# Output projection by column halves, the first tile's ranks, picks and gather moved up, residual sums opened inside expert 0

## The reference

```
x = x + merged @ w_o                                  # 1024 x 1024
h2 = rmsnorm(x, norm2_g)
logits = h2 @ w_router + b_router                     # 32 experts
top_v, top_i = top_k(logits, 4); gates = softmax(top_v)
for each expert e, for the tokens that chose it:
    gu = h2 @ w_gate_up[e] + b_gate_up[e]             # 1024 x 2048
    act = (clip(gu[1024:], -7, 7) + 1) * g * sigmoid(1.702 * g),  g = min(gu[:1024], 7)
    x += gates * (act @ w_down[e] + b_down[e])        # 1024 x 1024
out = rmsnorm(x, final_g)
```

## Time and profile before

| what | value |
|---|---|
| time, median of 3 runs | 1134.14 us (1133.83 to 1134.21) |
| the profiled execution's own time | 1134.09 us |
| span of its trace | 1132.3 us, mean granted TensorE clock 0.991 |
| PE busy | 1091.9 us, 96% of the span |
| PE weight loads | 482.5 us, 43% |
| DVE, ACT, POOL busy | 223.8, 125.4 and 30.3 us |
| moved by DMA | 434.61 MB, mean 384 GB/s |
| SP's queue | 430.33 MB, 90.1% of what 16 engines can do in the span |
| PE idle for a load of up weights | 20.2 us, 14 times |

### The profile page before, as it was taken

How to read it: one execution, slowest core, us unless ns; L and a number is a source line. 1 busy time by engine, 2 the same in 40 slices (tenths; PEclk the granted TensorE clock), 3 DMA queues, 4 the chain that set the end, 5 groups by cost and what they waited for, 6 DMA issues and landing times.

```text
span 1132.3 us, 12526 instructions
## 1 busy us (share of the span) xinstructions
PE 1091.9 (96%) x5278; PEld 482.5 (43%) x5279; DVE 223.8 (20%) x549; ACT 125.4 (11%) x271; POOL 30.3 (3%) x43
## 2 busy tenths in 40 slices
PE   7999999999999999999999999999999999999996
PEld 5858887443333333333333333333333333333332
DVE  1264213331111111111111121111111111111112
ACT  1053111210000000000000010000000000000001
POOL 1250000000000000000000000000000000000000
PEclk9999999999999999999999999999999999999999
DMA  9934366399999999999999999999999999999995
GB/s 362 411 144 168 130 222 233 144 396 421 432 432 432 429 431 433 431 432 433 432 431 431 435 428 429 439 428 429 438 428 431 435 429 431 434 429 431 417 421 232
DMA packets 31484, 434.61 MB, mean 384 GB/s; under 512 B 6944, under 2 KB 7200, under 8 KB 9440
## 3 DMA queue, kind: packets, MB, share of 16 engines
q1 hardware_dynamic: 26960, 430.33, 90.1%
q10 hardware_dynamic: 4496, 3.87, 1.1%
HBM read 433.14 MB, written 1.05 MB: 383 GB/s over the span
## 4 chain that ended last, share of the span: by engine, by line
PE 65%; DMA 32%; DVE 1%; ACT 1%; issue 0%; POOL 0%; DVEq 0%; SPq 0%; POOLq 0%
DMA ring<-in_up 32%; PE ps L1352 26%; PE ps L1366 11%; PE ps L1172 5%; PE ps L1300 3%; PE ps L1374 3%; PE ps L1186 2%; PE ps L1249 2%; PE ps L1061 2%; PE ps L1361 2%; PE ps L1116 1%; PE ps L1080 1%; PE ps L1051 1%; PE ps L1336 1%; PE ps L1330 1%; PE ps L1089 1%
## 5 line engine op out<-in xcount | busy, mean ns | idle before, releaser
L1352 PE MATMUL ps<-ring,work 128*64 128x512 f32 x2048 | 470.7, 605 | 20.2 <-DMA ring<-in_up 20.2
L1352 PEld LDWEIGHTS ps<-ring,work 128*64 128x64 f32 x2048 | 141.8, 138 | 317.8 <-issue 283.8
L1366 PE MATMUL ps<-ring,work 128*64 128x512 f32 x1024 | 226.8, 595 | 1.6 <-DVE work L977 1.6
L918 DVE TENSOR_SCALAR work<-ps 128x512 f32<-128x512 f32 x32 | 22.1, 691 | 698.1 <-PE ps L1352 698.1
L1366 PEld LDWEIGHTS ps<-ring,work 128*64 128x64 f32 x1024 | 70.6, 137 | 133.7 <-issue 128.0
L1300 PEld LDWEIGHTS ps<-work 128*128 128x128 f32 x512 | 61.8, 191 | 24.0 <-issue 22.7
L1300 PE MATMUL ps<-work 128*128 128x128 f32 x512 | 70.3, 281 | 0.5 <-DVE work L904 0.5
L1374 PE MATMUL ps<-work 64*128 64x512 f32 x264 | 65.6, 615 | 0.7 <-ACT work L658 0.7
L1172 PE MATMUL ps<-work,ring 128*128 128x256 f32 x256 | 56.6, 379 | 0.0
L631 ACT ACTIVATE work<-ps 128x256 f32<-128x256 f32 x33 | 12.7, 383 | 355.5 <-PE ps L1336 355.5
L1172 PEld LDWEIGHTS ps<-work,ring 128*128 128x128 f32 x256 | 48.5, 190 | 6.6
(11 more groups left out here) (157 smaller groups left out, 520.9 us busy)
## 6 DMA issues: line engine op xcount, KB each, us to landing
ring<-in_up SPq DMA_DIRECT2D x52, 4096.0 KB, 45.2
ring<-in_down SPq DMA_DIRECT2D x26, 4096.0 KB, 44.1
ring<-in_up SPq DMA_DIRECT2D x48, 1024.0 KB, 10.8
ring<-in_down SPq DMA_DIRECT2D x24, 1024.0 KB, 10.6
ring<-in_front SPq DMA_DIRECT2D x22, 1024.0 KB, 17.2
ring<-in_front SPq DMA_DIRECT2D x2, 832.0 KB, 7.5
ring<-in_x SPq DMA_DIRECT2D x2, 512.0 KB, 4.2
ring<-in_x ACTq DMA_DIRECT2D x1, 1024.0 KB, 4.8
```

The source lines that it names most:

```text
L918: return dve.tensor_scalar(up_c, ps[:, UP, :], LIMIT, -LIMIT, ALU.min, ALU.max)
L1352: last = pe.matmul(ps[n * CAP:(n + 1) * CAP, bank, :], x, w[bank - GATE][:, n * BANK:(n + 1) * BANK], start=k == 0, stop=k == KT - 1, skip ...
L1366: last = pe.matmul(ps[n * CAP:(n + 1) * CAP, Y, :], lhs(actT, k), w[:, n * BANK:(n + 1) * BANK], start=k == 0, stop=k == KT - 1, skip_grou ...
```

## The change

1. `w_o` is packed by column halves: its first two slots hold half 0, four steps k each, the next two half 1. PE runs half 0 of tile 0, half 0 of tile 1, half 1 of tile 0, half 1 of tile 1. The transposes, the router's products and `add_parts(0)` stand between these passes, at new places, and DVE's and ACT's steps follow the new order: `x2_ready` now counts by half and then by tile. The first two slots of `w_o` are freed in the second pass, the other two in the fourth. The router's partial sums of tile 1 go to bank 0.
2. The counts of tile 0 are made after its own choice. DVE makes its places and picks (`first_picks(0)`) ahead of `choose(1)`, and PE gathers tile 0 ahead of the wait for tile 1's choice. Tile 1 follows with `first_picks(1)` and eight products. The halves of the gather change banks.
3. One `open_sums` stays ahead of the experts, three go into expert 0, behind its first three `up_tile`. `turn_gated(1)` moves from behind the second `up_tile` to behind the fourth, to another bank.
4. SP issues the first four loads of turn 1 ahead of the load of slot 23.

No product, copy or byte is added or taken away, except that the places and picks of the first round are made in two steps, each half as wide.

```diff
@@ pack_front
-    slots += list(rows_of(w_o, 2))
+    for half in range(2):
+        slots += list(rows_of(w_o[:, half * BANK:(half + 1) * BANK], 4))
@@ sync
+            for at in range(4):
+                fine_load(1, at)
             sp.wait_ge(opened, 1)
             expert_load(0, 23)
...
-            for at in range(RING):
+            for at in range(4, RING):
                 fine_load(1, at)
@@ vector
+            def first_picks(t):
+
+                dve.wait_ge(chosen_ready, t + 1)
+                dve.wait_ge(count_done, t + 1)
+                stepped(dve.scalar_tensor_tensor(out=struck[:, t, 0:E], in0=counts[:, t * E:(t + 1) * E], scalar=1.0, in1=chosen[:, t, :],
+                                                 op0=ALU.add, op1=ALU.mult))
+                step_wait()
+                stepped(dve.tensor_scalar(places[:, t, 0:E], struck[:, t, 0:E], -1.0, None, ALU.add))
+                step_wait()
+                for b in range(PAIR):
+                    last = dve.tensor_scalar(pick[:, t, b * CAP:(b + 1) * CAP], slots, places[:, t, b:b + 1], None, ALU.is_equal)
+                last.then_inc(pick_ready, 1)
+
             residual(0, 0)
+            take_x2T(0)
+            residual(1, 0)
+            take_x2T(1)
             residual(0, 1)
-            take_x2T(0)
-            dve.wait_ge(x2_sq, 2)
+            dve.wait_ge(x2_sq, 3)
             mean_square(0).then_inc(ms, 1)
+            dve.wait_ge(power, 4)
+            normed(0, 0)
+            normed(0, 1)
             choose(0)
-            residual(1, 0)
-            normed(0, 0)
-            take_x2T(1)
-            normed(0, 1)
             residual(1, 1)
+            first_picks(0)
             dve.wait_ge(x2_sq, 4)
             mean_square(1).then_inc(ms, 1)
             choose(1)
             normed(1, 0)
...
+            first_picks(1)
+            normed(1, 1)
@@ tensor
             def project(t, k, n):
-                w = slot(FIRST["wo"] + k // 2, 2, D)
-                return pe.matmul(ps[:, 4 + 2 * t + n, :], gateT[:, k, t * P:(t + 1) * P], w[:, k % 2, n * BANK:(n + 1) * BANK],
+                w = slot(FIRST["wo"] + 2 * n + k // 4, 4, BANK)
+                return pe.matmul(ps[:, 4 + 2 * t + n, :], gateT[:, k, t * P:(t + 1) * P], w[:, k % 4, :],
                                  start=k == 0, stop=k == KT - 1)
...
+            for k in range(KT):
+                last = project(1, k, 0)
+                if k % 4 == 3:
+                    last.then_inc(freed, 1)
+                if k == 3:
+                    turn_rows(0, 0)
...
@@ expert 0
-                        if static and e == 0 and k == 1:
+                        if static and e == 0 and k in (0, 1, 2):
+
+                            last = open_sums(*((0, 1), (1, 0), (1, 1))[k])
+                            if k == 2:
+                                last.then_inc(opened, 1)
+                        if static and e == 0 and k == 3:
 
                             pe.wait_ge(first_gates, 1)
-                            turn_gated(1).then_inc(first_ps, 1)
+                            turn_gated(1, Y).then_inc(first_ps, 1)
```

More of the change, by code:

```diff
@@ L398, in fine_load @@
                 expert_load(i, at)
-            for at in range(RING):
+            for at in range(4):
+                fine_load(1, at)
+            sp.wait_ge(opened, 1)
+            expert_load(0, 23)
+            for at in range(4, RING):
                 fine_load(1, at)
@@ L834, in residual @@
             def residual(t, n):
-                dve.wait_ge(*((wo_done, 1), (wo_done, 1), (wo_done, 2), (freed, through("wo")))[2 * t + n])
+                dve.wait_ge(*((wo_done, 1), (freed, FIRST["wo"] + 2), (wo_done, 2), (freed, through("wo")))[2 * n + t])
                 dve.tensor_tensor(xrow[:, t, n * BANK:(n + 1) * BANK], xrow[:, t, n * BANK:(n + 1) * BANK], ps[:, 4 + 2 * t + n, :],
@@ L918, in clamp_up @@
                 return dve.tensor_scalar(up_c, ps[:, UP, :], LIMIT, -LIMIT, ALU.min, ALU.max)
-            stepped(build_places(0))
-            step_wait()
-            build_picks(0, 0)
-            build_picks(1, 1).then_inc(pick_ready, 1)
-            normed(1, 1)
             for r in range(1, ROUNDS):
@@ L1232, in route @@
                     k = 4 * j + q
-                    last = pe.matmul(ps[q * E:(q + 1) * E, 4, 0:P], router_w[:, k, :], x2T[:, k, t * P:(t + 1) * P], start=j == 0, stop=j == 1)
+                    last = pe.matmul(ps[q * E:(q + 1) * E, (4, 0)[t], 0:P], router_w[:, k, :], x2T[:, k, t * P:(t + 1) * P], start=j == 0, stop=j == 1)
                 if j == 1:
@@ L1247, in project @@
             def project(t, k, n):
-                w = slot(FIRST["wo"] + k // 2, 2, D)
-                return pe.matmul(ps[:, 4 + 2 * t + n, :], gateT[:, k, t * P:(t + 1) * P], w[:, k % 2, n * BANK:(n + 1) * BANK],
+                w = slot(FIRST["wo"] + 2 * n + k // 4, 4, BANK)
+                return pe.matmul(ps[:, 4 + 2 * t + n, :], gateT[:, k, t * P:(t + 1) * P], w[:, k % 4, :],
                                  start=k == 0, stop=k == KT - 1)
+            counts = ps[:, GATE, P:P + (TT + 1) * E]
             for k in range(KT):
-                if k % 2 == 0:
-                    arrived(FIRST["wo"] + k // 2)
+                if k % 4 == 0:
+                    arrived(FIRST["wo"] + k // 4)
                 pe.wait_ge(merged, k + 1)
-                for n in range(2):
-                    last = project(0, k, n)
+                last = project(0, k, 0)
                 if k == 0:
@@ L1301, in picked, with gather_first @@
                                  skip_group_check=True)
-            def gather_first():
-                for t in range(TT):
-                    for k in range(KT):
-                        if k % 4 == 0:
-                            pe.wait_ge(h2_ready, 2 * t + k // 4 + 1)
-                        last = picked((MIX, Y)[k // 4], k % 4, k, t, t == 0 and k % 4 == 0, t == TT - 1)
-                        if t == TT - 1 and k == 3:
-                            last.then_inc(gathered_low, 1)
-                last.then_inc(gathered, 1)
+            def gather_first(t, ks):
+                for k in ks:
+                    if k % 4 == 0:
+                        pe.wait_ge(h2_ready, 2 * t + k // 4 + 1)
+                    last = picked((Y, MIX)[k // 4], k % 4, k, t, t == 0 and k % 4 == 0, t == TT - 1)
+                return last
             def gather(k):
@@ L1377, in _ @@
             pe.wait_ge(pick_ready, 1)
-            gather_first()
-            open_sums(1, 1).then_inc(opened, 1)
+            gather_first(0, range(0, 2))
+            add_parts(1)
+            gather_first(0, range(2, 8))
+            pe.wait_ge(chosen_ready, 2)
+            pe.matmul(counts[:, E:2 * E], before, chosen[:, 1, :], start=False, stop=True, skip_group_check=True)
+            pe.matmul(counts[:, 2 * E:3 * E], ones, chosen[:, 1, :], start=False, stop=True, skip_group_check=True).then_inc(count_done, 1)
+            open_sums(0, 0)
+            pe.wait_ge(pick_ready, 2)
+            gather_first(1, range(0, 4)).then_inc(gathered_low, 1)
+            gather_first(1, range(4, 8)).then_inc(gathered, 1)
             pe.wait_ge(over_ready, 1)
```

79 lines of the change are left out of this document (37 added, 42 removed).

## The result

The changed kernel takes **1137.74 us** (median of 20 runs, 1135.04 to 1139.65), the kernel before 1134.12 us in the same session (20 runs, 1133.16 to 1138.27). The ratio is 1.0031, 95% interval 1.0025 to 1.0037: 3.6 us slower, where 0.8 us faster was forecast. It lies outside the forecast's range. The profiled execution took 1137.49 us.

The account below looks back on a forecast made before the run. The stream of expert weights bounds the kernel; expert 0 starts 2.4 us earlier, but pauses between its loads leave slot 4 of turn 1 landing 0.8 us earlier: 1134.09 - 0.8 = 1133.3 us, range 1131.7 to 1134.6 us.

Parts of the forecast that it names:

- What bounds the kernel: Second half: the stream of expert weights, 2.43 us a slot, sets the end, fixed where it becomes full near 240 us.
- Part 1: Output product by halves: two loads go out near 202 and 206 us; slot 22 lands about 231 instead of 234.6 us.
- Part 2: Front, router choices and gather: despite an added wait of 0.67 us, expert 0 starts at 230.4 us, 2.4 us earlier.
- Part 3: Sums in expert 0: 0.95 us each, so slots come free every 2.67 us and the stream pauses until 240.4 us.
- Part 4: First loads of turn 1: slot 4 lands at 250.4 instead of 251.2 us, 0.8 us gained, bounds 0.1 and 1.3.
- Behind it loads queue without a hole, before and after, so the end moves by what this landing moves.: Turn 1, behind slot 4's landing: the stream stays full, so the end shifts by as much as that landing.
- a hole between 251 and 310 us: Sign in the weight stream, behind slot 4's landing, that would show the forecast wrong.
- PE is then as late as before: 0.45 us late ... with no wait there: Expert 0: PE starts 2.4 us earlier, loses three times 0.95 us, ends 0.45 us late, still ahead of the stream.
- a second seam takes it back: Rival: slot 8 of turn 1, freed late, finds 3.1 us queued; a 0.7 us overlap cancels the gain: 1134.1 us, chance 0.19.
- TensorE clock: Rival: a front wait of about 2 us lowers PE's clock over gather and first tiles, 1.7 us: 1136.4 us, chance 0.08.
- some 650 us: Point in the run from which PE was said to wait for weights, its lead of slots used up.
- the clock's 0.08: Chance of the clock rival; half counted within 0.2% of before, the other half given as 0.05 slower.

Follow-up runs that it names:

- fill_late_free: fill with the loads of slots 7 and 8 of turn 0 held back until the third output-weight slot is free; 1134.04 us, ratio 0.9996.
- fill: Changed kernel without sums in expert 0: two fill PE's front waits, the last follows the gather, slot 23 loads ahead of turn 1; 1132.43 us, ratio 0.9985.
- after_warm: Changed kernel with three extra unused 128x512 products in PE's last wait for a landing; 1136.92 us, ratio 1.0023.
- front_only: Changed kernel with three residual sums back ahead of expert 0, behind the gather, and slot 23 loaded ahead of turn 1; 1135.10 us, ratio 1.0007.
- after: The changed kernel itself, against the kernel before; 1137.74 us, ratio 1.0031.
- after_busy_front: Changed kernel with an unused 256-column product ahead of each of PE's two waits at the front; 1137.05 us, ratio 1.0025.

## Why the prediction failed, point by point

**What bounds the kernel: right.** The stream of weights sets the end, then the tail. An earlier start of expert 0 moved nothing by itself.

**Part 1: right in its times.** The loads of slots 7 and 8 of turn 0 went out at 201.1 and 205.0 us (forecast 202 and 206), and slot 22, issued at 224.4 us, landed 7.9 us later, at 232.3 (forecast 231; before 234.6). That this was needed for a gain isn't shown: the profile of fill_late_free, without the early loads of slots 7 and 8, has the same times from P0 at slot 8 and at the last group as fill.

```profile
L363 SPq DMA_DIRECT2D ring<-in_down x1: 327/327/327, 224.4 to 224.4; - x1
```

**Part 2: right in kind, a quarter too large.** Expert 0 started at 230.21 us, forecast 230.4, but this execution's P0 was 0.76 us early. From P0 it is 39.6 us against the forecast 39.0 and 41.4 before: 1.8 us won, not 2.4. The mis-sized term is the first: `add_parts(0)` came at P0 + 29.6 us, not 29.0, since the product with six narrow groups in it is longer than the sum of its parts: the changes between them took some 0.6 us together, forecast 0.1. The three waits were 0.41 us, 0.69 us and, for the second picks, none. The DVE chain behind kept its length (the choice from 220.64 to 221.83 us, forecast 1.20):

```profile
220.64 0.25 DVE L870 SCALAR_TENSOR_TENSOR work<-ps,sums,work 128x32 f32<-128x32 f32 x1 [2.36 <-PE ps L1258]
...
221.65 0.18 DVE L881 TENSOR_SCALAR work<-work 128x32 f32<-128x32 f32 x1
```

**Part 3: a quarter too small.** A sum between two tiles costs 1.2 us (2.93 less 1.73), not the 0.95 us of one behind the gather. The four loads went out 2.93 us apart, not 2.67.

**Part 4: the number met by luck, and it was the wrong number.** Slot 4 landed at 250.6 us, forecast 250.4:

```profile
L363 SPq DMA_DIRECT2D ring<-in_up x1: 328/328/328, 243.2 to 243.2; - x1
...
DMA to landing us min/median/max: 7.4/7.4/7.4
```

But this execution's P0 was 0.76 us early. From P0 slot 4 landed at 60.0 us, forecast 59.0, before 59.8: 0.2 us late instead of 0.8 us early. The fourth load was issued at P0 + 50.3 us, forecast 49.0, by what parts 2 and 3 had wrong. The 8 us from P0 + 42 us, before and after:

```profile
233.40:241.40 8.00, 8.00 (x40) 2.57 (x38) 2.60 (x14) 0.38 (x1) 0.00 (x0) 1.00 0.95 340
232.60:240.60 8.00, 8.00 (x30) 2.05 (x28) 0.30 (x2) 0.00 (x0) 0.00 (x0) 1.00 0.91 316
```

So both kernels dip at the first loads of turn 1, and the changed one dips more. The step that failed is the next one: "Behind it loads queue without a hole, before and after, so the end moves by what this landing moves." Slot 5 landed 3.7 us behind slot 4, slot 8 was issued with 3.0 us left in the queue, and slot 9 landed 3.4 us behind slot 8. There was a hole between 251 and 310 us, which the text had named as what would prove it wrong: the far end moved some 1.8 us more than slot 4's landing. By its landings it wasn't so before either. Slot 5 had landed at 253.6 us (issued at 243.9), and slot 6 landed at 257.1 us:

```profile
L362 SPq DMA_DIRECT2D ring<-in_up x1: 328/328/328, 246.1 to 246.1; - x1
...
DMA to landing us min/median/max: 11.0/11.0/11.0
```

That is 3.5 us behind slot 5, with 7.5 us in the queue at its issue. The landing of one load behind a dip says little: slot 5 of the changed kernel landed at 254.3 us, 3.7 us behind slot 4, inside a window of 421 GB/s (250 to 256 us, above). The bytes moved by windows show when the stream is full.

**"PE is then as late as before: 0.45 us late ... with no wait there": the lateness was the price.** It was 1.8 us from P0 (0.6 less won in part 2, 0.75 more lost in part 3, 0.45 forecast). PE itself indeed waited for nothing there. But PE's progress sets SP's issues, and slot 8 is issued when PE says so.

**The rival "a second seam takes it back": the mechanism was right, its size and its chance were not.** It worked out 3.1 us left in the queue; 3.0 were measured. It then set 0.7 us against the gain and held the end at 1134.1 us. The traces show the dip to 341 GB/s, 1.5 us in the 8 us behind the issue, and slot 8 itself landed 0.4 us late from P0: 1.9 of the 2.0 us at the far end. I had subtracted 2.43 us from 4.6 and taken the 2.2 us left as enough in the queue; no row showed a queue of 3 us that held the rate.

**The rival "TensorE clock": right in kind, wrong in place and condition.** The forecast put the fall at the front, from a wait of about 2 us. At the front it fell in single executions, in after_warm after waits of 0.4 and 0.7 us. In the profiled executions of the changed kernel it fell at the tail, where PE waited 3.2 and 3.7 us instead of 2.1, for 1.7 and 2.8 us; in front_only it fell there after 2.13 us too, so the longer wait isn't shown to be the reason. I had taken as a price but not asked where the last such wait stands, behind which nothing can hide it.

**Two smaller readings.** PE's first wait for weights ended at 698.2 us; the "some 650 us" is the issue of the load that it waited for. And half of the clock's 0.08 is 0.04, so the chances add up to 0.83, 0.13 and 0.04.

Together: forecast -0.8; profiled +1.1 of stream at the last wait (+2.0 at the far end from P0, less an early P0), +1.7 of clock, +0.6 in the stores and short waits of the tail. The stream's part is shown by experiment, some 2 us by the medians; the clock's part in single executions; the medians don't divide what is left of the 3.6 us.

## What to carry to other kernels

Where a stream of loads bounds a kernel, look for every place at which the consumer frees late, and read the queue there as the landing of the load ahead less the issue: a load that comes earlier ahead of such a seam gains nothing if the seam's own load comes later. The shortest queue alone doesn't name the seam (after has 0.1 to 1.8 us at slots 0 to 3 and 3.0 us at slot 8); what counts is the last seam whose issue comes later than before with too little queued. Work is not moved for nothing into a stretch that looks free of waits, if that stretch paces the issue of loads; the same sums cost nothing inside PE's waits for DVE and ACT, and 1.2 us each between tiles. Compare executions from a marker of their own, since their fronts start up to 1.5 us apart.

## What the hardware showed unexpectedly

- A load that joins a queue of 2.9 to 3.6 us slows the stream: 317 to 359 GB/s over 8 us instead of 416 to 422, with the share of busy DMA time still at 0.93 to 0.97.
- In single executions the granted clock fell to 0.60 and 0.50 after waits of 0.3 to 1.4 us among products of 32 and 128 columns, where every single wait was short. Behind PE's last wait for a landing it fell after 2.13 us (front_only), 3.17 and 3.71 us and didn't after 2.94 us (after_busy_front) and 3.55 us; in the kernel before it fell after 2.16 us and didn't after 2.14 us. What decides between them stays open.
- A float32 product of 512 columns costs 1.2 us between tiles of another shape, 0.95 us behind the gather.
